# Router from the unnormed residual, with the first task's rows scaled once they are gathered

## The chip, the cores and the metric

The kernel runs on one core of a Trainium2 chip. The metric is the time of one execution on the device, in microseconds. TensorE (PE) multiplies matrices, VectorE (DVE) and ScalarE (ACT) work element by element, GpSimd (POOL) here only issues transfers, SyncE (SP) issues the weight loads. Each engine has its own instruction queue and they wait for each other with semaphores.

## The reference

Two trunk layers of a diffusion backbone over 384 tokens of width 1024: one block of 128 prompt tokens (conditioned by `c_ctx`) and 256 latent tokens (conditioned by `c`). The part that matters here is the second half of layer 1:

```
xp = xp + g1 * merge_branches(...)                       # output projection, gated residual
h2 = rmsnorm(xp, norm2_g[l]) * (1.0 + sc2) + sh2          # sc2, sh2 differ for prompt and latent tokens
logits = (h2 @ w_router[i]).astype(F32)                   # 8 experts
top_v, top_i = lax.top_k(logits, TOP_K)                   # the two best for each token
top_w = jax.nn.softmax(top_v, axis=-1)
for e in range(N_EXP):
    y = y + gates[..., e:e + 1] * swiglu(h2, w_ex_gate[i, e], w_ex_up[i, e], w_ex_down[i, e])
```

rmsnorm divides a token by the root of the mean of its squares plus 1e-6 and multiplies by a gain. Everything is float32.

## The kernel before

Activations stay on the chip, turned: `xT` is the residual as 8 chunks of 128 channels by 384 tokens, `macc` a second array of that shape, `hhi` and `hlo` the high and low parts of the current input (a float32 product is made of three products of parts, `mm3`, L698 to L702). Weights come in slots of up to 128 x 2048 through six buffers; ScalarE copies each to its high part `whi` (`hi`, `expert_hi`), VectorE subtracts to get the low part `wlo` (`lo`, `expert_lo`), in rings of three.

The order of each engine's work is written out by hand in one block for each engine. Around the change:

- `out_projection` (L1088) on TensorE works in four quarters of 256 channels. After each, VectorE's `residual` (L2064) adds two chunks to `xT`; ScalarE squares them (`square`, L1410) into `macc`; VectorE sums them (`first_sum`, `second_sum`).
- `mean_squares(3)` (L752): TensorE sums squares over channels in one-column products, ScalarE takes the root (`root`), VectorE the reciprocal, TensorE spreads it over the partitions (`spread`). VectorE's `normalise(3)` and ScalarE's `modulate(3)` write h2 into `macc`, pair of chunks by pair. Beside it TensorE transposes `xT` to token rows (`residual_turned`) and ScalarE copies them to `xtok2`, which the end of the kernel needs.
- `router` (L1115 on TensorE, L2076 on VectorE): eight products with `macc` in four groups of 32 columns give partial logits; ScalarE copies them to `lrow`; products with `pick` add the groups and turn them. VectorE compares logits, TensorE turns the choice into positions (`pos_mm`), VectorE makes choice matrices `gat`, then the table of tasks. Meanwhile TensorE transposes h2 to rows, ScalarE copies them to `h2tok` and issues the transfer to the DRAM array `h2d` (L1808).
- A task is up to 128 tokens of one expert: 18 slots (`expert_task`), 12 for gate and up, 6 for down. Nine tasks run here, eight in a loop and the last apart. The first task's rows come by product with `gat` (`first_rows`, L1145); ScalarE takes the high part (L1683), VectorE the low (`first_low`, L2199). Those of every later task come by an indirect transfer from `h2d` on GpSimd (`gather`, L666), issued while the task before runs; TensorE transposes them right after its slot 12 (`rows_turned`, L1210), in order with its other work. GpSimd's loop is entered after the wait for `h2_out` (L675).
- GpSimd also loads `rows` (gate and final gain broadcast to all partitions, L658, L661).

Of the kernel before, what the change touches and what calls it, by code (L numbers as in the profile page):

```python
# [136 lines left out]
def prefix_step_kernel(nc, a, outs, const):  # L137
    y_prompt, y_sample, new_dk, new_dv, new_wk, new_wv = outs
    ctx = ExitStack()
    with ctx:  # L140
# [45 lines left out]
        pick = place("pick", [32])  # L186
        adarow = place("adarow", [256])
# [57 lines left out]
        h2tok = at("h2tok", BLK * D, hhi_at, shape=[BLK, D])  # L245
# [11 lines left out]
        gat = at("gat", T, oraw_at + 4096, shape=[BLK, P])  # L257
        ehh = at("ehh", KF * P, oraw_at + 5632, F32R, [KF, P])
# [64 lines left out]
        h2_tr, h2_ev, h2_out, slotc_in, pos_mm = sem("h2_tr"), sem("h2_ev"), sem("h2_out"), sem("slotc_in"), sem("pos_mm")  # L323
# [16 lines left out]
        g2d = nc.dram_tensor("g2d", [KD, 2 * P], F32).ap()  # L340
        yd = nc.dram_tensor("yd", [MAX_TASKS * P, D], F32).ap()
# [274 lines left out]
        def _(pool):  # L616
# [58 lines left out]
            pool.wait_ge(h2_out, 16)  # L675
# [21 lines left out]
        def _(pe):  # L697
# [54 lines left out]
            def mean_squares(i):  # L752
# [17 lines left out]
                if i == 3:  # L770
                    residual_turned(0)
# [4 lines left out]
                if i == 3:  # L776
                    for b in (1, 2):
                        residual_turned(b)

            def residual_turned(b):  # L780

                if b == 0:
                    pe.wait_ge(res_done, 16)
# [304 lines left out]
            def out_projection(l):  # L1088
# [15 lines left out]
                for j in range(2, 4):  # L1104
                    n = out_slot(l, j)
                    if l == 1 and j == 2:
                        pe.wait_ge(merge_done, 6 * DEPTH)
                        for v in range(2):
                            mm = pe.transpose(ps[0:KD, 7, v * P:(v + 1) * P], mods[:, 1, G2:G2 + KD, v], ident)
                        mm.then_inc(g2_tr, 1)  # L1110
                    pe.wait_ge(lo_done, split_count(n + 1))
# [3 lines left out]
            def router():  # L1115
                pe.wait_ge(wrout_in, 16)
                for k in range(KD):
                    if k % 2 == 0:
                        pe.wait_ge(chain_m, 8 * 3 + k + 2)
                        pe.wait_ge(mod_done, 4 * 3 + k // 2 + 1)  # L1120
# [3 lines left out]
                mm.then_inc(rt_rows, 1)  # L1124
                pe.wait_ge(lrow_ready, 1)
                for b in range(BLK):
                    mm = pe.matmul(ps[:, 7, T + b * N_EXP:T + (b + 1) * N_EXP], lrow[:, b * P:(b + 1) * P], pick[:, 0:N_EXP],
                                   start=True, stop=True)
                mm.then_inc(rt_done, 1)

                for b in range(BLK):
                    pe.wait_ge(x2_ev, b + 1)
                    for k in range(KD):
                        mm = pe.transpose(ps[:, 2 * b + k // 4, (k % 4) * P:(k % 4 + 1) * P],
                                          macc[:, k, b * P:(b + 1) * P], ident)
                    mm.then_inc(h2_tr, 1)
# [8 lines left out]
            def first_rows():  # L1145

                pe.wait_ge(gat_ready, 1)
                pe.wait_ge(h2_ev, BLK)
                for k in range(KD):
                    for b in range(BLK):  # L1150
                        mm = pe.matmul(ps[:, 2 + k // 4, (k % 4) * P:(k % 4 + 1) * P], h2tok[:, b, k * P:(k + 1) * P],
                                       gat[:, b, :], start=(b == 0), stop=(b == BLK - 1))
# [187 lines left out]
            for l in range(DEPTH):  # L1340
# [9 lines left out]
                mean_squares(2 * l + 1)  # L1350
                if l == 0:
                    units()
# [1068 lines left out]
```

## Time and profile before

| | |
|---|---|
| time, median of 3 runs (lowest, highest) | 1526.55 us (1524.73, 1528.66) |
| profiled execution: time, span | 1526.82 us, 1524.7 us |
| mean granted TensorE clock | 0.994 of 2.4 GHz |
| TensorE busy | 1483.0 us, 97% |
| VectorE, ScalarE busy | 939.4 us (62%), 783.2 us (51%) |
| HBM traffic | 224 GB/s over the span |

Times of instructions are microseconds from the start of the span. "L700" is line 700 of the kernel before. An engine's busy time counts overlapping instructions once; TensorE's matmuls are pipelined, so one that lasts 0.39 us can be followed 0.23 us later. A matmul of float32 data (not of high and low parts) appears as two instructions. Idle time names in brackets what ended it.

### The profile page before, as it was taken

To read this page: it belongs to the slowest core of one execution; us is meant where nothing else is said; L and a number is where in the kernel's file an instruction comes from. 1 tells how busy PE (TensorE), PEld (TensorE's weight loads), DVE (VectorE), ACT (ScalarE), POOL (GpSimd) and SP (SyncE) were. 2 spreads that over 40 slices of the span, in tenths; PEclk is the share of its full clock that TensorE was granted. 3 is DMA by queue.
4 is the path that set the end of the run, shared out by engine and by line. 5 is a ranking of instruction groups with operands and counts; after the bars stand their busy time and mean duration, and the time that the engine had idled before them with its cause. 6 is when DMAs were issued, how large, how long until landed. Compare 5 with 4: busy or idle time off the path is not lost.

```text
span 1524.7 us, 22132 instructions
## 1 busy us (share of the span) xinstructions
PE 1483.0 (97%) x8674; PEld 1305.9 (86%) x8674; DVE 939.4 (62%) x1078; ACT 783.2 (51%) x895; POOL 53.6 (4%) x54
## 2 busy tenths in 40 slices
PE   7999999999999999999999999998999999999997
PEld 5788969699899999997889696998888888888875
DVE  4542275655554354346522755556898898988988
ACT  4443264543432242235333544435778778787875
POOL 0100000000000000001000000000000000000002
PEclk9999999999999999999999999999999999999999
DMA  9844265567763454265333554535899999999994
GB/s 327 268 169 160 96 223 165 166 220 239 245 166 100 135 138 125 93 223 163 124 111 111 166 166 139 166 116 192 321 371 390 376 374 377 377 390 373 374 380 163
DMA packets 236186, 342.33 MB, mean 225 GB/s; under 512 B 8661, under 2 KB 157054, under 8 KB 235854
## 3 DMA queue, kind: packets, MB, share of 16 engines
q1 hardware_dynamic: 227552, 313.32, 60.2%
q0 software_dynamic: 6496, 24.69, 4.4%
q10 hardware_dynamic: 2062, 3.24, 0.6%
q8 instruction: 56, 0.92, 0.3%
q14 instruction: 20, 0.16, 0.0%
HBM read 325.74 MB, written 15.47 MB: 224 GB/s over the span
## 4 chain that ended last, share of the span: by engine, by line
PE 88%; DVE 6%; ACT 3%; DMA 1%; SPq 1%; issue 1%; DVEq 0%; ACTq 0%
PE ps L700 26%; PE ps L702 25%; PE ps L701 25%; DVE wlo L2209 2%; PE ps L717 2%; PE ps L942 1%; PE ps L976 1%; ACT whi L1636 1%; PE ps L960 1%; SPq L475 1%; ACT ebuf L1544 1%; PE ps L1174 1%; DMA raw<-in_w_in_dram 1%; PE ps L798 1%; PE ps L727 1%
## 5 line engine op out<-in xcount | busy, mean ns | idle before, releaser
L700 PE MATMUL ps<-hhi,whi 128*128 128x384 f32 x824 | 276.6, 336 | 0.3 <-DVE hidlo L2306 0.3
L702 PE MATMUL ps<-hhi,wlo 128*128 128x384 f32 x824 | 275.3, 334 | 0.0
L701 PE MATMUL ps<-hlo,whi 128*128 128x384 f32 x824 | 275.3, 334 | 0.0
L1828 DVE TENSOR_TENSOR wlo<-raw,whi 128x2048 fp32r<-128x2048 f32 x65 | 148.7, 2289 | 179.5 <-ACT whi L1371 167.9
L2209 DVE TENSOR_TENSOR wlo<-raw,whi 128x2048 fp32r<-128x2048 f32 (+1 forms) x81 | 179.1, 2228 | 27.4 <-ACT whi L1636 26.9
L1636 ACT ACTIVATE whi<-raw 128x2048 fp32r<-128x2048 f32 (+1 forms) x81 | 150.6, 1868 | 49.4 <-PE ps L702 49.2
L2209 DVE TENSOR_TENSOR wlo<-mraw,whi 128x2048 fp32r<-128x2048 f32 (+2 forms) x81 | 160.7, 1993 | 16.3 <-ACT whi L1636 15.8
L700 PE MATMUL ps<-whi,xgh 128*128 128x512 f32 (+1 forms) x432 | 164.0, 380 | 4.4 <-DVE wlo L2209 3.7
L1636 ACT ACTIVATE whi<-mraw 128x2048 fp32r<-128x2048 f32 (+2 forms) x81 | 136.6, 1687 | 50.9 <-PE ps L702 50.7
L702 PE MATMUL ps<-whi,xgl 128*128 128x512 f32 (+1 forms) x432 | 161.0, 373 | 0.0
L701 PE MATMUL ps<-wlo,xgh 128*128 128x512 f32 (+1 forms) x432 | 160.5, 372 | 0.0
L700 PEld LDWEIGHTS ps<-hhi,whi 128*128 128x128 f32 x824 | 154.7, 188 | 2.4 <-issue 2.0
L701 PEld LDWEIGHTS ps<-hlo,whi 128*128 128x128 f32 x824 | 154.7, 188 | 0.3
L702 PEld LDWEIGHTS ps<-hhi,wlo 128*128 128x128 f32 x824 | 154.7, 188 | 0.0
L1371 ACT ACTIVATE whi<-raw 128x2048 fp32r<-128x2048 f32 x61 | 116.5, 1912 | 73.1 <-PE ps L702 58.8
L700 PE MATMUL ps<-whi,hhi 128*128 128x512 f32 (+1 forms) x285 | 108.8, 382 | 3.9 <-issue 2.0
L2292 DVE TENSOR_TENSOR wlo<-raw,whi 128x2048 fp32r<-128x2048 f32 (+1 forms) x36 | 76.1, 2113 | 57.9 <-ACT whi L1617 57.9
L702 PE MATMUL ps<-whi,hlo 128*128 128x512 f32 (+1 forms) x285 | 106.1, 372 | 0.0
L701 PE MATMUL ps<-wlo,hhi 128*128 128x512 f32 (+1 forms) x285 | 106.0, 372 | 0.0
L700 PEld LDWEIGHTS ps<-whi,xgh 128*128 128x128 f32 x432 | 81.1, 188 | 20.1 <-issue 6.0
L1617 ACT ACTIVATE whi<-raw 128x2048 fp32r<-128x2048 f32 (+1 forms) x36 | 63.8, 1772 | 54.4 <-PE ps L702 54.4
L702 PEld LDWEIGHTS ps<-whi,xgl 128*128 128x128 f32 x432 | 81.1, 188 | 11.8
(348 smaller groups left out, 2498.4 us busy)
## 6 DMA issues: line engine op xcount, KB each, us to landing
raw<-in_w_ada_dram SPq DMA_DIRECT2D x62, 512.0 KB, 5.4
raw<-in_w_ex_up_dram SPq DMA_DIRECT2D x27, 1024.0 KB, 7.3
raw<-in_w_ex_down_dram SPq DMA_DIRECT2D x27, 1024.0 KB, 5.9
raw<-in_w_gate_dram SPq DMA_DIRECT2D x48, 512.0 KB, 4.6
raw<-in_w_in_dram SPq DMA_DIRECT2D x44, 512.0 KB, 6.1
raw<-in_w_ex_gate_dram SPq DMA_DIRECT2D x18, 1024.0 KB, 7.0
mraw<-in_w_ex_gate_dram SPq DMA_DIRECT2D x18, 1024.0 KB, 7.8
mraw<-in_w_ex_down_dram SPq DMA_DIRECT2D x18, 1024.0 KB, 8.2
```

The source lines that it names most:

```text
L475: sp.dma_start(dst[i], src[i]).then_inc(side_in[EARLY_BUF[n]] if n in EARLY_BUF else raw_in[n % RING], 16)
L700: pe.matmul(out, s[0], m[0], start=first, stop=False, **kw)
L701: pe.matmul(out, s[0], m[1], start=False, stop=False, **kw)
L702: return pe.matmul(out, s[1], m[0], start=False, stop=last, **kw)
L717: mm = pe.matmul(ps[32 * j:32 * j + 32, bank, 0:256], sil32[:, k, 30 - 2 * i:62 - 2 * i], w[:, k, :], start=(i == 0 and k < 4), stop=(i == ...
L727: mm = pe.matmul(ps[32 * j:32 * j + 32, 7, 0:256], sil32[:, k, 30 - 2 * i:62 - 2 * i], w[:, k, :], start=(i == 0 and k < 4), stop=(i == la ...
L1371: act.activation(whi[:, n % RING, :], raw[:, n % RING, :], copy).then_inc(hi_done, 1)
L1617: act.activation(whi[:, s % RING, 0:used], raw[:, s % RING, 0:used], copy).then_inc(hi_done, 1)
L1636: act.activation(whi[:, m % RING, 0:E_USED[m]], mraw[m % MRAW][:, 0:E_USED[m]], copy).then_inc(hi_done, 1)
L1828: dve.tensor_tensor(wlo[:, n % RING, :], raw[:, n % RING, :], whi[:, n % RING, :].bitcast(F32), ALU.subtract).then_inc(lo_done, 1)
L2209: dve.tensor_tensor(wlo[:, m % RING, 0:E_USED[m]], mraw[m % MRAW][:, 0:E_USED[m]], whi[:, m % RING, 0:E_USED[m]].bitcast(F32), ALU.subtrac ...
L2292: dve.tensor_tensor(wlo[:, s % RING, 0:used], raw[:, s % RING, 0:used], whi[:, s % RING, 0:used].bitcast(F32), ALU.subtract).then_inc(lo_d ...
```

## The change

The logits are computed from `xT` itself. With r the reciprocal root of a token, logit = r * (xT . (w_router * gain)) + (shift . w_router). `wr2` holds the router weights times the gain for latent and prompt tokens; the shift's part is computed during the output projection (`shrt`, `shlog`). The sum of squares comes as a ninth column of the same products, with `onec`, which is one in column 8. `mean_squares(3)`, `root(3)`, `normalise(3)` and `modulate(3)` are gone. The first task's rows are gathered from `xtok2`, with r in the choice matrix, prompt and latent rows in separate banks; ScalarE and VectorE then apply gain and shift on chunks of 128x128 (`hmod`). For the other tasks GpSimd first writes the shift rows to `h2d`; VectorE computes `xtok2 * r * gain` for three blocks inside the first task (after its slots 3, 4 and 5) and GpSimd adds them to `h2d` by an accumulating transfer, ahead of its loop. VectorE's first task is therefore written out ahead of its loop.

```diff
 # GpSimd
-            pool.wait_ge(g2_ready, 1)
+            pool.wait_ge(g2_ready, 2)
+            pool.dma_start(m2d, modrow[0:KD, :]).then_inc(g2_out, 16)
             pool.dma_start(g2d, adarow[0:KD, :]).then_inc(g2_out, 16)
             pool.wait_ge(o_ready, 3 * DEPTH)
-            pool.wait_ge(g2_out, 16)
+            pool.wait_ge(g2_out, 32)
+            for i in (2, 3, 0, 1):
+                pool.dma_start((shrow if i < 2 else murow)[:, i % 2, :].rearrange("p (k c) -> p k c", k=KD),
+                               m2d.rearrange("(o k) (i c) -> i o k c", o=1, i=4)[i].to_broadcast([P, KD, P])
+                               ).then_inc(rows_in, 16)
+            pool.wait_ge(rows_in, 16 * 4)
+            pool.dma_start(h2d[0:P, :], shrow[:, 1, :]).then_inc(h2_out, 16)
+            pool.dma_start(h2d[P:T, :].rearrange("(b p) d -> p b d", p=P),
+                           shrow[:, 0, :].unsqueeze(1).to_broadcast([P, 2, D])).then_inc(h2_out, 16)
...
-            pool.wait_ge(h2_out, 16)
+            pool.wait_ge(h2_out, 32)
+            pool.wait_ge(h2_rows, BLK)
+            pool.dma_start(h2d.rearrange("(b p) d -> p b d", p=P), h2tok[:, :, :], accum_op=ALU.add).then_inc(h2_out, 16)
+            pool.wait_ge(h2_out, 48)
             pool.wait_ge(yd_out, 32)
 # TensorE, out_projection, layer 1, ahead of quarter 2 and of quarter 3
+                            pe.transpose(ps[0:KD, 6, v * P:(v + 1) * P], mods[:, 1, SH2:SH2 + KD, v], ident)
+                            pe.transpose(ps[0:KD, 6, (2 + v) * P:(3 + v) * P], amul[:, 1, 1, :, v], ident)
...
+                        for k in range(KD):
+                            g = 32 * (k % 4)
+                            mm = pe.matmul(ps[g:g + 32, 5, 0:2], wrout[:, k, :], mods[:, 1, SH2 + k, :], start=(k < 4),
+                                           stop=(k >= 4), tile_position=(0, g))
...
+                        for v in range(2):
+                            mm = pe.matmul(ps[:, 6, v * N_EXP:(v + 1) * N_EXP], shrt[:, v:v + 1].to_broadcast([P, P]),
+                                           pick[:, 0:N_EXP], start=True, stop=True)
 # TensorE, router
-                    mm = pe.matmul(ps[g:g + 32, 7, 0:T], wrout[:, k, :], macc[:, k, :], start=(k < 4), stop=(k >= 4),
-                                   tile_position=(0, g))
+                    for v, t in ((0, slice(P, T)), (1, slice(0, P))):
+                        mm = pe.matmul(ps[g:g + 32, 7, t], wr2[:, v, k, :], xT[:, k, t], start=(k < 4 and v == 0),
+                                       stop=(k in (6, 7) and v == 1),
+                                       tile_position=(0, g))
...
+                pe.wait_ge(sqs_done, SQS[3])
+                squares(ssum[:, 0, :], 0)
+                pe.wait_ge(sq_done, SQ0[3] + 4)
+                squares(macc[:, 6, :], 32, True)
+                pe.wait_ge(res_done, 16)
+                raw_logits(7)
+                pe.wait_ge(sq_done, SQ0[3] + 5)
+                squares(macc[:, 7, :], 0, True).then_inc(rt_rows, 1)
                 for b in range(BLK):
+                    if b == 1:
+                        pe.wait_ge(lrow_ready, 1)
+                        for c in range(BLK):
+                            mm = pe.matmul(ps[:, 7, T + c * 9:T + (c + 1) * 9], lrow[:, c * P:(c + 1) * P], pick[:, 0:9],
+                                           start=True, stop=True)
+                        mm.then_inc(rt_done, 1)
+                    if b == 2:
+                        pe.wait_ge(wr2_ready, 2)
+                    residual_turned(b)
+                pe.matmul(ps[:, 6, :], ident, cst[:, 0:512], start=True, stop=True)
 # TensorE, first_rows
-                pe.wait_ge(h2_ev, BLK)
+                pe.wait_ge(x2_ev, BLK)
+                pe.matmul(ps[:, 4, 0:P], ones[:, :], prompt[:, :], start=True, stop=True)
...
+                        mm = pe.matmul(ps[:, (2 if b else 0) + k // 4, (k % 4) * P:(k % 4 + 1) * P],
+                                       xtok2[:, b, k * P:(k + 1) * P], gat[:, b, :], start=(b < 2), stop=(b != 1))
 # ScalarE
+                    act.wait_ge(g2_out, 32)
                     act.activation(lrow[:, :], ps[:, 7, 0:T], copy).then_inc(lrow_ready, 1)
+                    act.wait_ge(rt_done, 1)
+                    act.activation(rcol[:, 0, :], ps[:, 7, T + 8:T + 35:9], ACT.Sqrt, scale=1.0 / D, bias=epsc[:, 0:1]).then_inc(rms_done, 1)
...
-                act.wait_ge(h2_out, 16)
                 for h in range(2):
                     act.wait_ge((half_rows, xg_tr)[h], 1)
-                    act.activation(xgh[:, 4 * h:4 * h + 4, :].rearrange("p k c -> p (k c)"), ps[:, 2 + h, :], copy
-                                   ).then_inc(half_high, 1)
+                    for k in range(4 * h, 4 * h + 4):
+                        act.activation(hmod[:, k, :], ps[:, 2 + h, (k % 4) * P:(k % 4 + 1) * P], ACT.Identity,
+                                       scale=amul[:, 1, 1, k, 0:1], bias=mods[:, 1, SH2 + k, 0:1]).then_inc(half_mod, 1)
+                for h in range(2):
+                    act.wait_ge(h_mod, h + 1)
+                    act.activation(xgh[:, 4 * h:4 * h + 4, :], hmod[:, 4 * h:4 * h + 4, :], copy).then_inc(half_high, 1)
 # VectorE
+            def first_modulated(h):
+                dve.wait_ge(half_mod, 4 * h + 4)
+                ks = range(4 * h, 4 * h + 4)
+                for k in ks:
+                    x = dve.scalar_tensor_tensor(hmod[:, k, :], ps[:, h, (k % 4) * P:(k % 4 + 1) * P], amul[:, 1, 1, k, 1:2],
+                                                 hmod[:, k, :], ALU.mult, ALU.add)
+                link(x)
+                for k in ks:
+                    x = dve.scalar_tensor_tensor(hmod[:, k, :], ps[:, 4, 0:P], shdiff[:, k:k + 1], hmod[:, k, :], ALU.mult, ALU.add)
+                x.then_inc(h_mod, 1)
...
+            def normed_rows(b):
+                if b == 0:
+                    dve.wait_ge(rows_in, 16 * 7)
+                    dve.wait_ge(x2_tr, BLK)
+                dve.wait_ge(x2_ev, b + 1)
+                dve.scalar_tensor_tensor(h2tok[:, b, :], xtok2[:, b, :], rcol[:, 1, b:b + 1], murow[:, int(b == 0), :],
+                                         ALU.mult, ALU.mult).then_inc(h2_rows, 1)
...
+                    if s in (3, 4, 5) and isinstance(q, int):
+                        normed_rows(s - 3)
...
+                expert_task(0, True)
                 dve.wait_ge(pos_ready, 1)
                 last = dve.value_load(tasks[0:1, NQ:NQ + 1], min_val=N_EXP - 1, max_val=MAX_TASKS - 1)
-                with dve.Fori(0, last) as q:
+                with dve.Fori(1, last) as q:
                     expert_task(q, True)
```

On VectorE `router_weights` computes `wr2`, `slot1` and `shdiff` after quarter 1 of the projection; in `router` three scaled additions of `shlog` replace the copy of the logits, a choice row `prompt` is added, and `gat` gets the factor r. `first_modulated(0)` stands after the task table is done, `first_modulated(1)` between the low parts of the two halves.

## Rows read from the trace of the kernel before

**Rows 1.** The page, busy time of each engine over the span.
```profile
PE 1483.0 (97%) x8674; PEld 1305.9 (86%) x8674; DVE 939.4 (62%) x1078; ACT 783.2 (51%) x895; POOL 53.6 (4%) x54
```
**Rows 2.** Chain of waits: start, us, what; layer 1's attention, then projection to experts.
```profile
930.04 1.92 PE ps L717 x32
...
1043.93 0.75 DVE xT L2072 x2
...
1045.28 0.92 PE ps L765 x6
...
1049.33 0.96 DVE macc L1848
...
1069.24 0.49 PE ps L700
```
**Rows 3.** Windows: length, PE, PEld, DVE, ACT, POOL busy, PEclk, DMA share, GB/s.
```profile
1046.00:1050.00 4.00, 4.00 (x23) 4.00 (x24) 0.84 (x2) 1.29 (x2) 0.00 (x0) 0.59 0.01 2
...
1069.00:1118.00 49.00, 48.43 (x233) 41.17 (x234) 41.84 (x33) 36.35 (x28) 2.32 (x1) 1.00 0.96 349
```
**Rows 4.** Timeline of PE: start, us, instruction group, idle before.
```profile
228.61 0.85 PE L1006 MATMUL ps<-osq,ones 128*32 128x384 f32 x8
...
1056.14 0.84 PE L1122 MATMUL ps<-macc,wrout 128*32 128x384 f32 x4 [0.73 <-ACT macc L1449]
1057.58 0.83 PE L1127 MATMUL ps<-pick,lrow 128*128 128x8 f32 x6 [0.60 <-ACT lrow L1802]
...
1061.07 0.83 PE L1142 MATMUL ps<-selz,ones 128*128 128x32 f32 x6
1062.89 5.62 PE L1151 MATMUL ps<-gat,h2tok 128*128 128x128 f32 x48 [0.99 <-DVE gat L2099]
...
1103.55 1.04 PE L1166 MATMUL ps<-cst,xrow 128*128 128x128 f32 x8
```
**Rows 5.** Timeline of DVE: router, task table, first task and its end.
```profile
1058.45 0.18 DVE L2081 COPY rsm<-ps 128x24 f32<-128x24 f32 x1 [2.76 <-PE ps L1127]
...
1060.50 0.18 DVE L2092 TENSOR_SCALAR selz<-selz 128x24 f32<-128x24 f32 x1
...
1062.16 0.68 DVE L2099 TENSOR_SCALAR gat<-slotc,posx 128x128 f32<-128x128 f32 x3
...
1066.59 0.15 DVE L2125 CAST tasks<-tk 128x1 int32<-128x1 f32 x1
...
1068.31 0.69 DVE L2202 TENSOR_TENSOR xgl<-ps,xgh 128x512 fp32r<-128x512 f32 x1
...
1083.47 6.16 DVE L2209 TENSOR_TENSOR wlo<-raw,whi 128x2048 fp32r<-128x2048 f32 x3
...
1120.08 0.68 DVE L2253 COPY ysb<-ps 128x512 f32<-128x512 f32 x1
```
**Rows 6.** Groups by form, whole span: busy us, mean ns, idle before.
```profile
L2274 DVE SCALAR_TENSOR_TENSOR xtok<-xtok,fin,rows 128x1024 f32<-128x1024 f32 x3 | 3.9, 1285 | 0.1
L2072 DVE SCALAR_TENSOR_TENSOR xT<-ps,mods,xT 128x128 f32<-128x128 f32 x16 | 5.5, 341 | 0.0
L1449 ACT ACTIVATE macc<-macc,mods,amul 128x128 f32<-128x128 f32 x4 | 1.9, 479 | 0.0
```
**Rows 7.** Timeline of POOL: second task's indirect transfer, first task's store.
```profile
1091.19 2.32 POOL L666 DMA_INDIRECT xrow<-h2d,idxi  x1 [55.06 <-DVE idxi L2192]
1121.57 0.56 POOL L673 DMA_DIRECT2D yd<-ysb  x1 [28.06 <-DVE ysb L2253]
```
**Rows 8.** DMA issues of 1000 to 1110: queue, count, KB, us to landing.
```profile
h2d<-h2tok ACTq DMA_DIRECT2D x1, 1536.0 KB, 5.3
...
xrow<-h2d,idxi POOLq DMA_INDIRECT x1, 9.8
```
**Rows 9.** GpSimd's queue in 1126 to 1127 (packets, MB, share); line 673's landing.
```profile
q0 software_dynamic: 73, 0.25, 60.4%
...
DMA to landing us min/median/max: 6.3/6.4/6.6
```

More of the change, by code:

```diff
@@ L244, in prefix_step_kernel @@
         rows = at("rows", 3 * D, shared + 4 * SLOT * (MRAW - RING), shape=[3, D])
-        h2tok = at("h2tok", BLK * D, hhi_at, shape=[BLK, D])
+        h2tok = at("h2tok", BLK * D, xT_at, shape=[BLK, D])
+        shrow = at("shrow", 2 * D, ohi_at, shape=[2, D])
+        modrow = at("modrow", 512, oraw_at)
+        over_at = shared + 4 * SLOT * (MRAW - RING) + 12 * D
+        murow = at("murow", 2 * D, over_at, shape=[2, D])
+        wr2 = at("wr2", 2 * KD * 32, over_at + 8 * D, shape=[2, KD, 32])
+        assert over_at + 8 * D + 8 * KD * 32 <= top[0] and ohi_at + 8 * D <= olo_at + 3072
+        hmod = at("hmod", D, scratch_at, shape=[KD, P])
         xtok2 = at("xtok2", BLK * D, hlo_at, shape=[BLK, D])
@@ L257, in prefix_step_kernel @@
         gat = at("gat", T, oraw_at + 4096, shape=[BLK, P])
+        slot1 = at("slot1", P, oraw_at + 2048)
+        shrt = at("shrt", 2, oraw_at + 3328)
+        prompt = at("prompt", P, oraw_at + 2560)
+        shlog = at("shlog", 2 * N_EXP, oraw_at + 3072, shape=[2, N_EXP])
+        shdiff = at("shdiff", KD, oraw_at + 3200)
         ehh = at("ehh", KF * P, oraw_at + 5632, F32R, [KF, P])
@@ L1125, in router, with raw_logits @@
-                pe.wait_ge(lrow_ready, 1)
-                for b in range(BLK):
[L1127 to L1136, printed above, removed]
+                def raw_logits(k):
+                    g = 32 * (k % 4)
+                    for v, t in ((0, slice(P, T)), (1, slice(0, P))):
+                        mm = pe.matmul(ps[g:g + 32, 7, t], wr2[:, v, k, :], xT[:, k, t], start=(k < 4 and v == 0),
+                                       stop=(k in (6, 7) and v == 1),
+                                       tile_position=(0, g))
+                    return mm
@@ new lines, in squares @@
+                def squares(part, g, last=False):
+                    return pe.matmul(ps[g:g + 32, 7, 0:T], onec[:, :], part, start=False, stop=last, tile_position=(0, g))
+                pe.wait_ge(wr2_ready, 1)
+                pe.wait_ge(res_done, 14)
+                for k in range(4):
+                    raw_logits(k)
+                for k in (4, 5):
+                    raw_logits(k)
+                pe.wait_ge(res_done, 15)
+                raw_logits(6)
+                pe.wait_ge(sqs_done, SQS[3])
@@ L2074, in residual, with router_weights @@
                     x.then_inc(res_done, 1)
+            def router_weights():
+                dve.wait_ge(wrout_in, 16)
+                for v in range(2):
+                    x = dve.tensor_tensor(wr2[:, v], wrout[:, :, :], amul[:, 1, 1, :, v:v + 1].to_broadcast([P, KD, 32]), ALU.mult)
+                x.then_inc(wr2_ready, 1)
+                dve.wait_ge(slotc_in, 16)
+                dve.tensor_scalar(slot1[:, :], slotc[:, P:2 * P], 1.0, None, ALU.add)
+                link(dve.tensor_tensor(shdiff[:, :], mods[:, 1, SH2:SH2 + KD, 1], mods[:, 1, SH2:SH2 + KD, 0], ALU.subtract))
             def router():
+                reciprocal_root(3)
+                dve.wait_ge(rstd_ready, 2 * DEPTH)
+                dve.wait_ge(wr2_ready, 2)
                 dve.wait_ge(rt_done, 1)
@@ L2136, in router @@
                 dve.memset(fin[:, 0, 2:3], 0.0).then_inc(yv_ev, 1)
-                for h in range(2):
-                    first_low(h)
+                first_low(0)
+                first_modulated(1)
+                first_low(1)
             def shares():
```

81 lines of the change are left out of this document (41 added, 40 removed).

## The prediction

> **What bounds the kernel now.** I read the page's busy times first: TensorE is busy for 97% of the span, VectorE for 62% [rows 1]. So time can only be won where TensorE's queue waits or does work that isn't a weight product. The chain of waits between the last product of the output projection and the first product of the experts is such a place [rows 2]: from 1043.91 to 1069.24, 25.3 us, in which the chain runs over the last residual, sums of squares, a root, normalising steps on VectorE (from 1049.33), router products, transposes, the selection, a gather by matmul and a split. The granted clock was 0.59 there from 1046 to 1050, 1.2 GHz for most of the stretch, after TensorE had run matmuls of one column (L765) up to 1046.2 [rows 2, 3]. Then I read the expert task that follows: over its 49 us TensorE was busy 48.43 and VectorE 41.84 of 49 [rows 3], so VectorE is second, with some 7 us spare. Last I read what the first task's end needs from elsewhere: the rows of the second task, which one indirect transfer fetches from h2d. It was issued at 1091.19 [rows 7], 9.8 us pass until it lands [rows 8], 1101.0, and TensorE's transposes of it began at 1103.55 [rows 4]. That transfer has 2.5 us to spare, no more.
>
> **Out projection.** Added to TensorE ahead of its last quarters: four transposes, 16 matmul instructions of two columns on 32-column tiles, four of eight columns. Tiled instructions went out at 1.92 / 32 = 0.06 us each [rows 2]; six instructions of eight columns took 0.83, latency with it [rows 4], which makes 0.12 each. So 4 x 0.11 + 16 x 0.06 + 4 x 0.12 = 1.9, less a little overlap: 1.8. All of it is on the path, since nothing else fills TensorE there: the projection ends at 1045.7. VectorE's wr2, slot1 and shdiff (some 1.1 us after quarter 1), ScalarE's two small copies and GpSimd's six extra DMAs are hidden by the projection's last 18 us of products; without that cover they would cost their 1 to 2 us. The broadcasts feed murow, needed only near 1080.
>
> **Router.** Removed: sums by matmul, first root, spread, four scaled/shifted pairs. Eight raw products (a 256 and a 128 part, two instructions each) and three products of squares need 8 x 4 + 6 = 38 instructions. Four column groups overlap: eight instructions of 384 columns took 0.85 (L1006) [rows 4], which is two passes of 0.32 in each group and the latency. Group 0 has k = 0, k = 4 and two squares, four such pairs: 4 x 0.64 + 0.2 = 2.8. They begin at 1045.7, when all but the last chunk of xT are ready; the last residual (0.75) [rows 2] and a square (some 0.5) come at 1047.0, before group 0 is free. The rows are done at 1048.5, where before it was 1056.98 (1056.14 + 0.84) [rows 4]: 8.5 us earlier. Then lrow 0.5, the small products 0.83 (behind eight transposes, 0.3 more), now a root 0.3, a reciprocal 0.2 and three short scalings 0.4: logits at 1051.1. The comparison is unchanged, from 1058.45 + 0.18 to 1060.68, 2.05 [rows 5]: selection at 1053.1, 7.5 earlier. Positions ended 1.2 behind it, at 1061.90 [rows 4], a little of that behind 24 transposes, which now are done before: 1.1, so 1054.2. Choice matrices: before 0.9 us [rows 5]; now one more and a second scalar, 1.4: 1055.6, 7.2 earlier than 1062.84. The three copies of xT's rows are done on ScalarE by 1053.4.
>
> **First task's rows.** The 48 instructions took 5.6 us [rows 4]; with the prompt's product the halves are done at 1058.6 and 1061.3. ScalarE now modulates 8 chunks: 128x128 with scale and bias took 479 ns each, overlapped by some 60 [rows 6], 1.7 a half: 1060.3 and 1063.0. The first half's low part then waits for VectorE: its selection tail still takes 4.0 us (1062.75 to 1066.74) [rows 5], until 1059.6; then eight scalar operations of 341 ns, 0.26 apart [rows 6], to 1062.5, the task lists (1066.74 to 1068.31, 1.6) to 1064.1, and the split 0.69 [rows 5]: first product 1064.9. Second half: eight more (2.1), ScalarE's copy 0.6, split 0.7: 1068.2, so slot 1 waits 0.6. Before, slot 1 began at 1069.24 + 2.72 = 1071.96. Here the change is 3.8 us ahead, much less than the 8.5 won at the router, because modulation on both engines now stands on the path. What is late next is VectorE's low part of the second half. Bounds: without a wait for the tail it is 5.0 ahead, with 128-wide operations that don't overlap 3.0.
>
> **VectorE in the first task.** Three operations of 128x1024 with a vector factor stand between its weight splits of slots 5 to 8. The nearest row is 1285 ns (L2274) [rows 6], 1.2 in sequence: 3.6. VectorE had no gap there before: three splits follow each other without idle from 1083.47 to 1089.63 [rows 5]. The end of the second split was 1087.9, 15.9 after slot 1; now 1068.2 + 15.9 + 3.6 = 1087.7 (say 1087.9) for the third row block. The ring of three gives TensorE back about half: I take 1.6 of stall. Without anything else TensorE would reach the transposes of task two at 1103.55 - 3.8 + 1.6 = 1101.4.
>
> **The accumulating transfer.** Here the sum turns. Before, h2d was written at 1062.3 by a plain transfer, in 5.3 us, with no weights in flight [rows 8], 23 us before anyone asked. Now it begins after 1087.9, on GpSimd's queue, amid weights that take all engines, and the indirect transfer is queued behind it on GpSimd by the wait for 48; on that, TensorE's whole queue waits. GpSimd's start after VectorE's signal: 0.8 (VectorE's copy ended at 1120.76, the store began at 1121.57) [rows 5, 7]. The transfer: no row of before accumulates. Lower end 5.3 (plain, quiet engines); a store of 0.5 MB on the same queue amid weights took 6.4, its packets starting some 3.4 after the issue and getting about 60% of the engines, 0.25 MB/us [rows 7, 9]. So 1.57 MB plain is 3.4 + 6.3 = 9.7. Upper end: every byte moved twice, 3.4 + 12.6 = 16. I take 11, near the plain one, since that row is on the right queue under the right load. Then the loop's entry, 1.2 (0.4 for a register load, 0.8 as for the store's start), and the indirect transfer's 9.6 to 9.8.
>
> 1087.9 + 0.8 + 11 + 1.2 + 9.6 = 1110.5. TensorE's transposes move from 1103.55 to 1110.5: +6.9 us, after which the remaining eight tasks are as before (a task's 48.5 us are TensorE's own). TensorE stands idle for some 9 us, and in that time the weights' delay is absorbed.
>
> A rule of the Trainium skill bears on the term of 11. Collectives: The Full Stack, "The bandwidth ceiling: the fold count and why AG ≠ RS ≠ AR", says that a transfer which adds is slower not for the addition but since it reads two sources. No run here shows that yet. By it the transfer would take the upper end, 16, and the sum would be +11.9, 1538.7; by the row of the plain store it is +5.6.
>
> **Sum.** The profiled execution took 1526.82 us (span 1524.7), 0.3 above the median of 1526.55. 1526.8 + 6.9 = 1533.7; forecast 1533.5.
>
> **Rivals.**
> (a) The adding transfer doubles its traffic, or more: 16 us or up, 1538 to 1542. For it: DMA is at 0.96 over the task [rows 3]. Against: the weights stop as soon as TensorE does.
> (b) The transfer is nearly as quick as on quiet engines, 5.3 to 7, and the indirect one also, since the rings drain while TensorE waits (8.5): 1087.9 + 0.8 + 6 + 1.2 + 8.5 = 1104.4, +0.9 us, 1527.5. What was won at the router is used up exactly.
> (c) The other side, faster. The place is slot 12: if the rows arrive before TensorE asks, the 2.2 us of the stage stay (1101.4 against 1103.55), and more if the first task starts earlier: modulation from PSUM at 0.28 a chunk instead of 0.42, some 1.2, and products of squares that overlap better, 0.8. Then 4 us are won, 1522.5. It decides by one point: third row block to landed rows in under 14.6 us, where I count 22.6 and the lower ends add up to 0.8 + 5.3 + 0.8 + 7.5 = 14.4. So it needs every lower end at once.
> (d) The clock falls during TensorE's stand of 9 us. In the stretch 1046 to 1050 it ran at the lower level for 3.3 us after little work [rows 3]; with wide products behind it, that costs half, 1.6. It goes on top of (a) or of the forecast: 1535.1. The 16 narrow matmuls in the projection could do the same there.
> (e) The added waits hold something earlier: GpSimd must land four broadcasts and two fills before its three old row broadcasts; if murow came after VectorE wants it, near 1080, all moves one for one. They are three steps, one behind the other, begun near 1035; at 5 to 10 us a step [rows 8] they end by 1065. 15 us of room, so I give it nothing.
>
> **Chances.** Forecast with or without (d) 0.45, its own range 1530 to 1537; (a) 0.20; (b) 0.24; (c) 0.11. A measurement of this kernel tells some 0.3% from no change, 4.6 us: faster means below 1522.0, slower above 1531.1. (c) lies half inside the band, yet the router's whole side may be mis-sized by 2 us: faster 0.10. Slower: (a), and most of the forecast's share, 0.60. The same: 0.30. Range: from 1523, (b) with an earlier start, to 1541.
>
> **What would show it.** In the profile after: the small products of logits begin near 1049.4 (router right); first expert product near 1065; three VectorE operations of 1.2 to 1.3 us between splits before 1088; the indirect transfer issued near 1101 instead of 1091; and an idle time of TensorE ahead of the transposes of task two, put down to that DMA, of 5 to 12 us. If that idle time is missing, the prediction is wrong in its main step, and the span then is the router's 2 to 4 us shorter. If it is longer than 13, the adding transfer is slower than any row here led me to think. Task length from the second on should stay at 48.5.

## The result and the profile after

The changed kernel takes 1541.74 us (median of 4 runs, 1539.95 to 1545.01), the kernel before 1525.78 beside it: a ratio of 1.0088 (95% interval 1.0073 to 1.0102). It is 0.9% slower, where the prediction said 0.5% (1533.5). The whole range of the prediction ended at 1541, the forecast's own at 1537. The profiled execution took 1539.95, span 1538.2, so 13.5 us more than the span before.

Three rows divide the span. The last residual product (VectorE) stands at the end of the output projection, the first expert product (TensorE) ends the stretch that the router's part of the change is about, and the transposes of the second task's rows (L1219) are where the other part ends. First VectorE's and then TensorE's timeline of the kernel after; the columns are start, duration, engine, line, operation, operands, and in brackets the idle time ahead and who ended it:

```profile
1045.82 0.74 DVE L2126 SCALAR_TENSOR_TENSOR xT<-ps,mods,xT 128x256 f32<-128x256 f32 x2 [2.35 <-PE ps L729]
1050.62 0.49 DVE L2149 SCALAR_TENSOR_TENSOR rsm<-ps,rcol,shlog 128x8 f32<-128x8 f32 x3
...
1052.99 0.18 DVE L2162 TENSOR_SCALAR selz<-selz 128x24 f32<-128x24 f32 x1
...
1054.76 0.86 DVE L2170 TENSOR_SCALAR gat<-slot,posx,rcol 128x128 f32<-128x128 f32 x3
...
1067.86 0.69 DVE L2286 TENSOR_TENSOR xgl<-hmod,xgh 128x512 fp32r<-128x512 f32 x1 [0.70 <-ACT xgh L1738]
...
1087.69 1.27 DVE L2293 SCALAR_TENSOR_TENSOR h2tok<-xtok,rcol,murow 128x1024 f32<-128x1024 f32 x1
```

```profile
1049.34 0.73 PE L1182 MATMUL ps<-pick,lrow 128*128 128x9 f32 x6
...
1055.99 5.52 PE L1204 MATMUL ps<-gat,xtok 128*128 128x128 f32 x48
1065.20 0.79 PE L727 MATMUL ps<-whi,xgh 128*128 128x512 f32 x1 [3.68 <-DVE xgl L2286]
...
1115.01 1.97 PE L1219 MATMUL ps<-cst,xrow 128*128 128x128 f32 x8 [12.10 <-DMA xrow<-h2d,idxi]
```

From the last residual to the first expert product it was 25.31 us before (1043.93 to 1069.24, [rows 2]) and is 19.38 now. Of this 5.9 us, 1.9 is spent on the longer projection, so the first product comes 4.0 sooner. Then from the first product to the end: 455.5 us before, 473.0 now, +17.5. The last row above holds most of that: TensorE idle for 12.10 us ahead of the transposes, where nothing waited before [rows 4]. GpSimd's timeline shows why:

```profile
1089.53 1.32 POOL L701 DMA_DIRECT2D h2d<-h2tok  x1 [36.15 <-DVE h2tok L2293]
1105.96 2.73 POOL L690 DMA_INDIRECT xrow<-h2d,idxi  x1 [15.11 <-issue]
```

The indirect transfer goes out at 1105.96 and not at 1091.19 [rows 7], behind an adding transfer that took 14.6 us from issue to landing. The answer on the tile h2tok gives that figure:

```profile
L701 POOL DMA_DIRECT2D h2d<-h2tok x1: 1316/1316/1316, 1089.5 to 1089.5; - x1
...
DMA to landing us min/median/max: 14.6/14.6/14.6
```

By "stand" this text means such an idle time of TensorE at slot 12. Two more losses are in the windows (busy time of each engine, granted clock, DMA share, GB/s; the last three rows with all engines, the first three of TensorE alone): TensorE's clock is 0.50, its lower level (1.2 GHz), in slot 0, and again during and behind the stand.

```profile
1064.00:1066.00 2.00, 0.80 (x2) 0.72 0.97 367
1066.00:1068.00 2.00, 2.00 (x6) 0.50 1.05 409
1068.00:1070.00 2.00, 2.00 (x10) 0.92 0.61 225
```

```profile
1090.00:1104.00 14.00, 12.91 (x68) 11.22 (x66) 12.47 (x11) 8.06 (x7) 0.85 (x1) 1.00 1.04 283
...
1115.00:1117.00 2.00, 1.99 (x9) 1.99 (x10) 0.00 (x0) 0.00 (x0) 0.00 (x0) 0.50 1.05 387
1117.00:1119.00 2.00, 2.00 (x6) 1.52 (x6) 0.86 (x1) 1.02 (x1) 0.00 (x0) 0.50 1.05 383
```

The first of these last three rows is the adding transfer at work: the DMA engines are fully taken (1.04), yet move 283 GB/s. In the kernel before they moved 383 to 393 GB/s at shares of 1.02 to 1.08 with weights alone (1106 to 1120).

### The profile page after: what moved, and what is told of

It reads as the page before. It is cut to its first block, busy times and chain, and to the rows that moved or that the text cites. A ratio compares the mean times of both kernels' runs of the same rounds, so it can differ in the third digit from the quotient of the medians.

```text
span 1538.2 us, 22153 instructions
## 1 busy us (share of the span) xinstructions
PE 1485.0 (97%) x8676; PEld 1307.8 (85%) x8676; DVE 942.8 (61%) x1095; ACT 779.1 (51%) x894; POOL 60.7 (4%) x62
## 4 chain that ended last, share of the span: by engine, by line
PE 87%; DVE 6%; ACT 2%; DMA 2%; issue 1%; ACTq 0%; SPq 0%; POOLq 0%; DVEq 0%
PE ps L727 25%; PE ps L729 24%; PE ps L728 24%; DVE wlo L2300 2%; PE ps L744 2%; PE ps L962 1%; ACT whi L1686 1%; PE ps L996 1%; PE ps L980 1%; DMA h2d<-h2tok 1%; PE ps L818 1%; ACT ebuf L1594 1%; PE ps L1227 1%; DMA xrow<-h2d,idxi 1%; PE ps L1219 1%
```

## The experiments

Kernels ran on several chips, each beside the kernel before; the ratio to it is what the timed runs give, whose executions lie 2 to 9 us apart for one kernel. Their profiled executions can be read more closely. The table cuts each in two at the first expert product, which takes out the differences of whatever lies ahead. "Start" is from the last residual product to the first expert product, "rest" from there to the end of the span, both worked out from the timelines and the span.

| kernel | ratio to before (95%) | start us | rest us | idle ahead of the transposes |
|---|---|---|---|---|
| before | 1 | 25.3 | 455.5 | 0 |
| after | 1.0088 (1.0073-1.0102) | 19.4 | 473.0 | 12.1 |
| e1 plain | 1.0048 (1.0032-1.0064) | 19.4 | 469.0 | 7.1 |
| e2 no transfer | 0.9992 (0.9979-1.0005) | 21.1 | 458.7 | 0 |
| e3 no rows | 0.9975 (0.9964-0.9987) | 19.4 | 457.1 | 0 |
| e4 later | 1.0053 (1.0037-1.0070) | 21.1 | 470.1 | 2.0 |
| e5 by block | 1.0061 (1.0047-1.0076) | 19.4 | 466.9 | 5.5 |
| e6 GpSimd | 1.0043 (1.0028-1.0059) | 22.4 | 462.3 | 0 |
| e7 fill | 1.0091 (1.0074-1.0108) | 21.1 | 472.5 | 12.2 |
| e9 GpSimd, fill | 1.0039 (1.0025-1.0054) | 23.2 | 463.8 | 0 |
| e10 early | 0.9984 (0.9973-0.9995) | 20.5 | 458.9 | 0 |
| e11 early, fill | 0.9996 (0.9986-1.0006) | 20.5 | 458.7 | 0 |

A further cut, at the transposes of the second task's rows, divides the rest (e4 has them elsewhere). From there to the end of the span it is 421.1 to 421.7 us in every kernel without a stand, the kernel before among them (1103.55 to 1524.7), and 423.1 to 423.6 in those with one. So the low clock behind the stand costs 2.0 us, and nothing else of the difference lies there. From the first expert product to the moment at which TensorE asks for the rows it is 34.3 us before, 37.7 after, 37.6 in e2 and 35.8 in e3. With this the 13.5 us of span are divided: -4.0 since the first product comes sooner, +3.4 from there to slot 12, +12.1 of stand, +2.0 behind it.

The 3.4 has two parts. The twelve products of slot 0 took 2.83 us before and 4.29 after (4.33 in e3), most of them at the low clock: 1.5. VectorE's row products are the rest, as e3 against e2 shows (1.7). In e1, e4, e6 and e9 slot 0 took 5.27 to 5.28, a further 1.0, which no edit explains; that is to be kept in mind for their "rest".

The starts of 21.1 and 19.4 differ in one thing: in some executions the clock falls while TensorE makes the first task's rows. The row of the 48 products takes 5.52 us in e3 and 7.15 in e2:

```profile
1055.70 5.52 PE L1201 MATMUL ps<-gat,xtok 128*128 128x128 f32 x48
```

```profile
1055.45 7.15 PE L1202 MATMUL ps<-gat,xtok 128*128 128x128 f32 x48
```

It is not tied to an edit: e2 and e3 are alike up to there. So 1.7 us of a "start" is put down to chance here; with one trace of each kernel that can't be tested further.

**e1 to e4.** e1 makes the third transfer a plain write; e2 takes it out; e3 takes out VectorE's products too; e4 moves the transposes.

```diff
-            pool.dma_start(h2d..., h2tok[:, :, :], accum_op=ALU.add).then_inc(h2_out, 16)
+            pool.dma_start(h2d..., h2tok[:, :, :]).then_inc(h2_out, 16)          # e1
-            pool.dma_start(h2d..., h2tok[:, :, :], accum_op=ALU.add).then_inc(h2_out, 16)
-            pool.wait_ge(h2_out, 48)                                            # e2, e3
-                    if s in (3, 4, 5) and isinstance(q, int):
-                        normed_rows(s - 3)                                      # e3
-                    if i == 0 and more:
+                    if i == 3 and more:                                         # e4, TensorE
                         rows_turned(q * 16 + 16)
-                    if s == 13 and more:
+                    if s == 15 and more:                            # e4, ScalarE and VectorE
```

> The changed kernel with the same third transfer to the h2d array as a plain write instead of an adding one (left out: the shift rows, which the plain write replaces). Same bytes written, same issue, same start at 1089.5, same gather behind it. Theory A (the adding is what is slow): the transfer lands some 9.7 us after its issue, as the plain one of the kernel before, and not 14.6; the gather, the transposes and the end come 5 us sooner, so the stand at slot 12 shrinks from 12.1 to about 7 and the run takes about 1535. Theory B (any write of 1.5 MB beside the weight stream takes so long): it still lands after 14 to 15 us, and the run takes 1539 to 1541.

The transfer landed after 10.5 us and not 14.6, TensorE stood 7.1 and not 12.1, the rest is 4.0 us shorter (the stand gives 5.0, slot 0 took 1.0 more). Adding costs 4.1 us on 1.57 MB; theory B is out, theory A's 9.7 was 0.8 short. During that transfer the engines moved 406 GB/s, against 283:

```profile
1091.00:1101.00 10.00, 10.00 (x57) 9.32 (x57) 9.51 (x9) 8.38 (x7) 0.00 (x0) 1.00 1.02 406
```

The rows of GpSimd's queue (packets, MB, share of the 16 engines) show what adding asks of the engines, first of the changed kernel over 1088 to 1105, then of e1 over 1088 to 1103:

```profile
q0 software_dynamic: 400, 1.57, 48.9%
```

```profile
q0 software_dynamic: 400, 1.57, 26.8%
```

The same 400 packets took 0.489 x 17 = 8.3 us of all engines with the adding and 0.268 x 15 = 4.0 without. So their time doubled, as rival (a) of the prediction had it. The time to landing grew by less, since the adding packets also held more of the engines while they ran, 8.3 of some 11 us against 4.0 of some 8.

> The changed kernel without the adding transfer (left out: the normed rows of the later tasks; the gather reads the shift rows that are there already); VectorE's three row products stay, and the gather waits for the index alone, ready at 1091.2. Theory A (the stand at slot 12 is this transfer and the gather behind it): no idle time is left ahead of the transposes, TensorE's clock stays up there, and the run loses 12.1 us of stand and about 2 us at the low clock: about 1526. Theory C (the part ahead of slot 12 is itself slower than before, by VectorE's products and the low clock in slot 0): it stays 3 us or more over the kernel before, 1529 or more. Theory D (the gather by itself would be late): a stand of several us stays at slot 12.

The ratio is 0.9992, the rest 14.3 us shorter than in the changed kernel. 12.1 of it is the stand, 2.0 the low clock behind it, 0.1 lies ahead. So theory A holds, and D is out, since nothing stands at slot 12. C's time is out too, as the run is not 3 us over before, but what C says is in the trace: the part from the first product to slot 12 is 3.3 us longer than before (37.6 against 34.3). The earlier first product hides it in the total.

> As the kernel without the adding transfer, and also without VectorE's three row products in slots 3 to 5 of the first task (left out: the normed rows of the later tasks). It prices the products: if they hold up TensorE as predicted (a stall of 1.6 us), it is 1.6 us faster than the kernel with them, about 1524.5, and this is what the router part of the change is worth, some 1 to 2 us against the kernel before. If VectorE has slack there, no difference (1526) .

The rest is 458.7 with VectorE's products and 457.1 without: 1.6 us, the size predicted. The timed runs say 2.6, within their spread. So the router's side by itself is worth 0.25% (2.0 to 5.5 us, by the interval).

> The changed kernel with TensorE's transposes of the next task's rows after slot 15 in place of slot 12 in every task, and ScalarE's and VectorE's work on them in slot 15 in place of 13. Nothing else moves, the adding transfer and the gather run as they do. Theory A (TensorE loses time only because it stands for these rows at slot 12): three slots of 3.6 us lie between, so of 12.1 us of stand 1 to 2 remain, the clock stays up: about 1527. Rival (the stand was a cover for something else that is late, weights above all, which then arrive late in slots 13 to 15; or the later transposes hold up slot 0 of each of the later tasks): 1532 or more, with idle time before the matmuls of slots 13 to 17 or of the next slot 0.

This expectation failed, and it is the most useful of the misses. The stand did shrink to 2.0 us and the clock stayed at 1.00, but the rest fell by only 2.9. The waits of TensorE, first of e4 from 1122 on, then of the changed kernel, then e4's around the stand (who waited for whom, total, times, longest):

```profile
PE ps L727 <- DVE wlo L2300: 10.6, 9, 1.2
```

```profile
PE ps L727 <- DVE wlo L2300: 3.7, 9, 1.0
```

```profile
PE ps L1219 <- DMA xrow<-h2d,idxi: 2.0, 1, 2.0
PE ps L727 <- DVE wlo L2300: 1.8, 1, 1.8
```

Each of the eight later tasks now loses 1.2 us in place of 0.3 at its first slot, 6.9 us in all (the ninth wait, of 1.0, is in both): ScalarE copies the new rows (1.03 us) and VectorE splits them just before the weights of slot 0 are due. My edit was charged eight times for a stand that comes once. And 1.8 us of weights are late where the stand had covered them: ScalarE waited there for the transfers of the down weights. 12.1 + 2.0 - 2.0 - 1.8 - 6.9 = 3.4, less 1.0 for the longer slot 0 makes 2.4, against 2.9 measured; the sum is good to half a microsecond.

**e5 to e7, e9.** e5 cuts the adding transfer by block. e6 lets GpSimd make the rows and writes them plainly; the two shift fills, VectorE's products and the waits that go with them are left out there. e7 fills TensorE's idle time ahead of slot 0; e9 is e6 with e7.

```diff
-            pool.wait_ge(h2_rows, BLK)
-            pool.dma_start(h2d..., h2tok[:, :, :], accum_op=ALU.add)...
+            for b in range(BLK):                                                # e5
+                pool.wait_ge(h2_rows, b + 1)
+                pool.dma_start(h2d[b * P:(b + 1) * P, :], h2tok[:, b, :], accum_op=ALU.add)...
+            for b in range(BLK):                                                # e6
+                pool.tensor_scalar(h2tok[:, b, :], xtok2[:, b, :], rcol[:, 1, b:b + 1], None, ALU.mult)...
+                pool.tensor_tensor(h2tok[:, b, :], h2tok[:, b, :], murow[:, int(b == 0), :], ALU.mult)...
+                pool.tensor_tensor(h2tok[:, b, :], h2tok[:, b, :], shrow[:, int(b == 0), :], ALU.add)...
+            pool.dma_start(h2d..., h2tok[:, :, :])...
                 mm.then_inc(xg_tr, 1)
+                for _ in range(4):                                              # e7
+                    pe.matmul(ps[:, 5, :], ident, cst[:, 0:512], start=True, stop=True)
```

> The changed kernel with the adding transfer cut into three, one for each block of 128 rows, each issued when VectorE has made that block (1081.6, 1085.6 and 1089.0) in place of one issue after the third. Same bytes, same adding. Theory A (the stand at slot 12 counts the transfer's 14.6 us from its start, so that only its last third must stand behind the third product): a third takes some 5 us, the last lands near 1096, the gather some 10 us later at 1106, and of the 12.1 us of stand 3 to 4 remain; the weights, which lose the same DMA time to the adding packets, come some 2 us late: about 1531 to 1533, a ratio to the kernel before of 1.003 to 1.004. Rival (three transfers serve each other's queue no faster, or each costs its own start and landing): the last lands after 1101 and the ratio stays at 1.006 or more.

The stand fell to 5.5 us and the rest by 6.1, so the direction is A's; the timed ratio of 1.0061 is at the rival's mark. Each block landed later than worked out: the three took 7.4, 9.0 and 9.6 us from issue to landing, where I had 5, and the indirect transfer went out 11.5 us after the third was issued (1092.12 to 1103.62). The third's later time by itself, 1092.12 and not 1089, says nothing: in this execution all lies 2.7 us later from the first expert product on, and behind that product it was issued at the same distance as the whole transfer in the changed kernel (24.2 and 24.3 us). Three transfers on one queue don't make the last one a third as long.

> The changed kernel with the normed rows made by GpSimd (nine operations of 128x1024, times root, times mu row, plus shift row) from 1054 on, in place of VectorE's three products, and one plain transfer of them in place of the two shift fills and the adding one. Theory A (stand by the adding transfer at 1089, and VectorE's products on TensorE's path): if GpSimd's operation takes 2 to 3 times VectorE's 1.28 us, the rows are ready by 1073 to 1090 and landed some 10 us later, the gather is not later than in the kernel before, nothing stands at slot 12, and VectorE's 2.5 us between the last two kernels without the transfer is won as well: ratio 0.998, about 1524. Rival 1 (GpSimd and VectorE hinder each other at memory, so that the router's and the first task's operations grow): 2 us or more over that, with longer VectorE operations between 1054 and 1090. Rival 2 (GpSimd needs over 4 us for one operation): rows later than 1090 and a stand at slot 12 as large as now.

Rival 1 came true. GpSimd took 2.85, 2.34 and 2.35 us for the first block, and VectorE's operations beside them grew. VectorE's timeline of e6:

```profile
1060.11 1.16 DVE L2191 TENSOR_TENSOR owner<-owner,by_task 128x120 f32<-128x120 f32 x1
...
1063.12 2.20 DVE L2201 CAST tasks<-tk 128x15 int32<-128x15 f32 x1
```

The same operations took 0.28 (L2185) and 0.17 (L2195) in the kernel after. The cast ended at 1065.32, as the GpSimd operation beside it did (1062.95 + 2.34 = 1065.29). GpSimd's operations grew too, to 5.41 us beside the long splits. The stand is gone, and so it is 10.7 us of rest better than the kernel after, 6.9 us by the ratios, but the start is 3 us longer and the first task 3.6 us over e2.

> The changed kernel with four more matmuls of 512 columns (an unused product, 0.85 us each at full clock) behind the choice of the first task's rows, where TensorE has 3.7 us of idle time ahead of slot 0. Theory E (slot 0 runs at 1.2 GHz for 3 us because of this idle time): the clock stays at 1.00 there, slot 0 ends 1.3 us sooner, but the transfer, the gather and the stand at slot 12 hang on VectorE's products, which are bound by slots 2 to 5 and come 1.3 us sooner too: ratio 1.008, about 1.3 us under the changed kernel. Rival (the clock falls anyway, or what bounds slots 0 to 2 is VectorE's and ScalarE's work on the weights): no difference, 1.0088.

The clock stayed at 1.00 from 1062 up to the stand, and slot 0 ran at the full level, in 3.46 us and not 4.29. Only 0.5 us of rest came of it, and the ratio shows none. TensorE's timeline of e7 tells why: it waits for VectorE's low parts instead, in both halves.

```profile
1067.02 0.49 PE L727 MATMUL ps<-whi,xgh 128*128 128x512 f32 x1 [0.28 <-DVE xgl L2288]
1070.48 0.49 PE L727 MATMUL ps<-whi,xgh 128*128 128x512 f32 x1 [0.46 <-DVE xgl L2288]
```

> The kernel with GpSimd's rows and the four filling matmuls together. If both theories hold, nothing stands at slot 12 and slot 0 runs at full clock: ratio 0.997, 1.3 us under the one with GpSimd alone. If the filling only moves the wait to the weights, it equals the one with GpSimd alone.

It equals e6 within both intervals. It doesn't test the filling as meant, though: after the filling TensorE still waited 2.5 us for VectorE, and the clock fell all the same (0.52 over 1068 to 1070, slot 0 in 5.27 us).

**e10, e11.** e2 shows that the stand hangs on the adding transfer alone, so it should be enough to start it sooner. VectorE waits for ScalarE three times between 1059 and 1072 in the changed kernel (0.7 to 0.9 us); e10 puts the products there. It also waits for fewer of the earlier row transfers. e11 adds three filling matmuls and reads the index a slot sooner.

```diff
+                for b in range(BLK):                              # e10, e11
+                    x = dve.tensor_tensor(by_task[:, b], ...)     # moved ahead
                 first_modulated(0)
 ...
                 first_modulated(1)
+                normed_rows(0)
                 first_low(1)
-                    if s in (3, 4, 5) and isinstance(q, int):
-                        normed_rows(s - 3)
+                    if s in (0, 1) and isinstance(q, int) and more:
+                        normed_rows(s + 1)
...
-                    dve.wait_ge(rows_in, 16 * 7)
+                    dve.wait_ge(rows_in, 16 * 4)
...
                 mm.then_inc(xg_tr, 1)
+                for _ in range(3):                                # e11
+                    pe.matmul(ps[:, 5, :], ident, cst[:, 0:512], start=True, stop=True)
...
-                    if s == 6 and more:
+                    if s == 5 and more:                           # e11
                         token_of(q + 2, 1)
```

> The changed kernel with VectorE's three row products moved ahead, into times when it waits for ScalarE (one between the second half's modulation and its low part, one in each of slots 0 and 1, in place of slots 3, 4 and 5), and the table work of the later tasks moved into the wait ahead of the first half's modulation, which brings the first product forward by up to 0.7 us. The adding transfer and all bytes stay. Theory A (only the time at which the adding transfer starts makes the stand at slot 12): the rows are ready by 1074, the transfer runs beside a DMA share of 0.5 to 0.8 and lands by 1090, the gather starts at the index (1091) and nothing stands at slot 12: the run loses 12.1 + 2 us against the changed kernel, ratio 0.999. Rival (the adding packets' DMA time is missing to the weights wherever it is put): slots 1 to 6 stand for weights instead, ratio 1.003 or more.

Nearly all of it came: the rows were ready at 1075.60, 1.6 us later than expected, the transfer was issued at 1076.16 and landed after 12.8 us, the indirect one went out at 1090.83, nothing stood at slot 12, and the rest is 14.1 us shorter than in the changed kernel. GpSimd's timeline of e10:

```profile
1076.16 1.32 POOL L701 DMA_DIRECT2D h2d<-h2tok  x1 [24.14 <-DVE h2tok L2294]
1090.83 1.14 POOL L690 DMA_INDIRECT xrow<-h2d,idxi  x1 [13.35 <-issue]
```

The adding bytes were the same, and the engines were no quicker on them: 254 GB/s at a share of 1.06 while it ran.

```profile
1077.00:1089.00 12.00, 11.31 (x52) 8.98 (x52) 11.70 (x13) 8.32 (x7) 0.48 (x1) 1.00 1.06 254
```

Between the first product and slot 12 TensorE waited 0.7 us for low parts of weights, in e2 0.8, so the rival is out. e10 is 0.16% faster than the kernel before (0.05 to 0.27%), which is at the edge of what can be told, and 1% faster than the changed kernel (0.9984 / 1.0088, each beside the kernel before on its own chip).

> The kernel with the early rows, with three filling matmuls behind the choice of the first task's rows (unused products that keep TensorE busy ahead of slot 0), and with the index of the next task's rows read in slot 5 in place of slot 6, so that the gather can start 3.4 us sooner. If slots 0 to 3 hang on TensorE's clock: 1 us under the kernel with the early rows (0.998). If they hang on VectorE, as the run with four filling matmuls says: the same, 0.999; the sooner index is worth something only if a stand is left at slot 12.

The rest is 458.7 against 458.9 and the ratio 0.9996 against 0.9984, with intervals that overlap: neither filling nor the sooner index is worth anything. The transfer ahead held the gather, not the index: the indirect transfer went out 14.7 us behind the adding one in both.

## Why the prediction came out as it did

The direction and the mechanism were right, the size was half: +6.7 us forecast, +13 to +16 measured. The time lies outside the forecast's own 1530 to 1537 and in the 1538 to 1542 of rival (a), which had a chance of 0.20. The transposes came 4.5 us later than in the sum (1115.0 and not 1110.5), of which 3.6 is the term of the adding transfer, and 2.0 of low clock came on top. By its own steps:

- **Out projection.** Predicted end 1045.7, measured 1045.82.
- **Router.** Predicted: logits 1051.1, selection 1053.1, positions 1054.2, choice matrices 1055.6. Measured by the ends of the rows above: 1051.11, 1053.17, 1055.62 for the first, second and fourth, and 1054.3 by the end of the position products. Counting the instructions of each column group by a row of before worked to 0.1 us.
- **First task's rows.** First product 1064.9, measured 1065.20; second half 1068.2, measured 1068.55. What I missed is the clock: slot 0 ran at 1.2 GHz after 3.7 us of idle time, so slot 1 began at 1069.49 and not at 1068.2, behind the clock and not behind the second half. The rest of e3 is 1.6 us longer than that of before with no other work in it, and slot 0 accounts for 1.5 of it (4.33 us against 2.83). With the clock up, e7's slot 0 still took 3.46 because of the later second half, so of the 1.5 some 0.6 would remain for VectorE; filling gave back 0.5 in the end.
- **VectorE in the first task.** Third row block 1087.9, measured 1088.96; it came 19.5 us behind the start of slot 1, as counted (15.9 + 3.6), so the 1.1 us are slot 1's lateness, the clock's again. 1.6 us of stall, e2 against e3 measured 1.6.
- **The accumulating transfer.** This is the step that was mis-sized. Its start: 0.8 predicted, 0.57 measured. The term of 11 is 14.6. The loop's entry: 1.2, measured 1.86 (1104.1 to 1105.96). Gather: 9.6, measured 9.05. With VectorE's 1.1 us later, the transposes come at 1115.0 and not 1110.5. I took the value near the plain row on the ground that that row had the right queue and load; e1 shows that row was right for a plain write (9.7 against 10.5), and that it says nothing of an adding one. Collectives: The Full Stack in the Trainium skill ("The bandwidth ceiling: the fold count and why AG ≠ RS ≠ AR") says of a collective's reduce step that it is slower because it reads two sources. This case agrees in kind: e1's pair is 10.5 against 14.6 us to landing, 4.0 against 8.3 us of the engines. That it is the second read that costs, no run here shows. By the doubling that the prediction's upper end took, landing would have been after 16. Rival (a) was nearer than the forecast, and right on the engines' time.
- **The clock in the stand**, rival (d), came on top, as foreseen: 1.6 predicted, 2.0 measured behind the transposes (423.2 us to the end, 421.1 before and in e2). The transposes' 11.5 us and these 2.0 are the whole 13.5 us between the spans.
- **Absorbed weights.** The text said that the stand absorbs the weights' delay. e4 bears that out: with the stand down to 2.0 us, 1.8 us of it shows.
- **Rival (c)** asked for every lower end at once. e10 removes the stand by another way, by starting the transfer 13.4 us earlier; then 12.8 us from issue to landing are no hindrance. It doesn't win (c)'s 4 us: the slow slot 0 and VectorE's products remain. What decided was when the transfer begins, not how fast it is. I priced the positions of VectorE's products as given and did not ask what a sooner place costs: e10's rest equals e2's to 0.2 us.

## What to carry to other kernels

Before pricing a new transfer, find its deadline and count back: the transfer that was issued at 1076.16 and took 12.8 us cost nothing at slot 12, the same one issued 13.4 us later cost 14.1. Put the work that feeds it into idle times of its engine ahead of the busy phase, even if these are a little short. A fix inside a loop is paid in every pass: compare it with the one pass in which the stand occurs.

## What the runs showed of the hardware

- Adding transfers slow the other traffic too: with all engines taken (share 1.04 to 1.06) they moved 283 and 254 GB/s, 406 with a plain write of the same bytes beside the same weights. The queue of the weights moved 1.98 MB in 13 us beside the adding transfer (1091 to 1104) and 2.05 MB in 9 us beside e1's plain one (1091 to 1100). The transfer itself took 14.6 (12.8 in e10) against 10.5 us, and 8.3 (8.5) against 4.0 us of all engines.
- GpSimd's issue of the adding transfer of 384 rows took 1.32 us, of the plain one 0.76.
- GpSimd's 128x1024 operations and VectorE's held each other up: a VectorE cast of 0.17 us took 2.20, until the GpSimd operation beside it ended, and the GpSimd operation that took 2.85 for the first block took 5.41 for the third.
- After 12.1 us of idle time TensorE's clock was 0.50 for some 4 us of full work (1115 to 1119); 5.5 us of idle time in e5 also brought it down (0.66 over 1106 to 1116); with 2.0 us in e4 it stayed at 1.00. Ahead of slot 0 an idle time of 3.7 us brought it to 0.50 in the kernel after, one of 2.5 us in e9 too. In e2 and e3, which are alike up to there, it fell during the first task's rows in the one and not in the other, which is worth 1.6 us of these products.
